# Decay sums of the first mixer: heads on partitions, one picking pass per head instead of four turnings

## The chip, the cores and the metric

The kernel runs on one core of one Trainium2 chip. The metric is the device time of one execution in microseconds (us), as the median over several runs. A core has a matrix engine (TensorE, PE in the rows, with its weight loads shown apart as PEld), a vector engine (DVE), a scalar engine (ACT), GpSimd (POOL), and queues that start transfers (SP).

## The reference, cut to what matters

The program is a chain of layers over 512 tokens of width 1024. The part that the change touches is the first layer's mixer (a state-space mixer with 32 heads in 4 groups, and 4 chunks of 128 tokens). For each head the cumulative sum of `da` inside a chunk is needed twice, as a column over the tokens `l` and as a row over the tokens `s`:

```python
dt = jax.nn.softplus(dt.astype(jnp.float32) + dt_bias.astype(jnp.float32))
a = -jnp.exp(a_log.astype(jnp.float32))
da = dt * a.reshape(g_, r_)
a_cs = jnp.cumsum(da, axis=2)
decay = segsum_exp(jnp.moveaxis(da, 2, -1))     # exp(cs[l] - cs[s]) for s <= l
cb = jnp.einsum('bclgn,bcsgn->bcgls', cm, bm)
y_diag = jnp.einsum('bcgls,bcgrls,bcsgrp->bclgrp', cb, decay, xdt)
```

## The kernel before

Every large product is made in float32 precision out of three passes of the faster fp32r type: each operand is split into a high part (rounded by ACT) and a low part (what is left, subtracted by DVE), and `passes` (the line L699 in the rows) issues high times high, high times low and low times high. A pass moves 512 columns against a stationary block of 128x128.

The first mixer runs at the start, in this order on PE. The input x is turned and split. The raw `dt` of all heads comes out of one block of 24 passes. For group 0 the block "B" follows, then `turn_dt` (four turnings that bring `dt` to tokens on partitions), the block "C", and `decay_sums`: eight small float32 matmuls that give `acs` (cumulative sums, tokens on partitions, a column for each head) and `tot` (chunk totals). Then come the four blocks of x features, four z tiles, the states and the outputs. Groups 1 to 3 do the same without the `dt` parts. The work order is written out by hand in `ssd_group(g)`; each engine runs its own list in order and waits on semaphores. The eight PSUM banks are handed out by the table in `Banks`: `claim` makes PE wait until the bank's last user has freed it.

Between the blocks PE fills in `spread_sums(j)`, one for each of the group's eight heads j: it turns a head's column of `acs`, repeated over 128 columns, four times (once for each chunk), so that PSUM holds the sums as a row on all 128 partitions. ACT's `exp_diff(j)` reads that bank and makes the exponentials of the differences, and DVE's `weights(j)` multiplies them by `CBm`. The places matter below: `spread_sums(0)` and `(1)` stand behind block x0 (and ahead of the sixteen turnings of `y_turn` in groups 1 to 3), `(2)` and `(3)` behind block x1, `(4)` behind block x3 and ahead of `x_turn(1)`, `(5)` behind `x_turn(1)` and ahead of z tile 0, `(6)` and `(7)` behind `x_turn(2)` and `x_turn(3)`. `x_turn` is four turnings.

`spread_sums(5)` claims bank 4, whose user before it is "CB", the products of B and C. DVE frees that bank when it has written `CBm` (L2258). On DVE this stands behind the conv taps of block x2 and the low parts of z, and those stand behind ACT's high parts of z (L1473).

At the start ACT's list is: softplus of `dt`, the exponential of `a_log` (L1494), the high parts of both x halves (L1482, eight pieces), three exponentials of the sums (L1498 to L1500), and the conv starts of B and C (L1526). DVE's list is: `da` (L2186), the copies of `acs` and `tot` (L2188, L2190), their difference (L2192), the low parts of both x halves (L2160, eight pieces), then the conv taps of B and C (L2227).

Of the kernel before, what the change touches and what calls it, by code (L numbers as in the profile page):

```python
# [7 lines left out]
ALU = mybir.AluOpType  # L8
ACT = mybir.ActivationFunctionType
AX = mybir.AxisListType  # L10
F32 = mybir.dt.float32
# [5 lines left out]
P = 128  # L17
T = 512
NT = T // P
# [16 lines left out]
S_HEADS, S_P, S_GROUPS, S_N = 32, 64, 4, 128  # L36
# [28 lines left out]
C_ID, C_TRI, C_ONE, C_MASK = 0, P, 2 * P, 3 * P  # L65
# [66 lines left out]
def build(nc, x, p, cst, par_a, par_b, w_ssd, w_dt, dt_bias, a_log, d_skip, w_ssd_out, w_hgrn, w_hgrn_out,  # L132
          ln_g, ln_b, w_mlp1, w_mlp2, w_gate, w_proj, mem, pos, w_mla, w_uq, w_ukv, w_mem, w_mla_out, fin_g, out):
    with ExitStack() as ctx:
# [16 lines left out]
        con = sb("con", [P, C_ALL])  # L151
# [4 lines left out]
        pT_base = nc.sbuf_base - 4 * DEPTH * KP * T  # L156
# [6 lines left out]
        psum = ctx.enter_context(nc.psum_tensor("psum", [P, 8, HALF], F32))  # L163
        tri = con[:, C_TRI:C_TRI + P]
# [4 lines left out]
        def carve(*shape):  # L169
            n = int(np.prod(shape))  # L170
            assert at[0] + n <= ARENA, (at[0], n)
            v = arena[:, at[0]:at[0] + n]
            at[0] += n
            if len(shape) == 2:
                v = v.rearrange("p (a b) -> p a b", a=shape[0])
            if len(shape) == 3:
                v = v.rearrange("p (a b c) -> p a b c", a=shape[0], b=shape[1])
            return v
# [20 lines left out]
        small = carve(5, S_HEADS)  # L199
        dbias, aneg, dskip, dtmp, _ = [small[:, n, :] for n in range(5)]  # L200
        dt_all = carve(NT, S_HEADS)
        da = carve(NT, S_HEADS)
        acs = carve(NT, S_HEADS)
        tot = carve(NT, S_HEADS)
        decay_end = carve(NT, S_HEADS)
# [16 lines left out]
        def part(name, first, *shape):  # L222
            return nc.alloc_sbuf_tensor_at(name, [P, *shape], F32R, offset=arena_base + 4 * first)

        def over(name, base, *shape):
            return nc.alloc_sbuf_tensor_at(name, [P, *shape], F32R, offset=base)
# [5 lines left out]
        z_his = [part(f"z_hi{n}", ring_first + n * KD * 256, KD, HALF) for n in range(2)]  # L232
        yT_hi = [over("yT_hi_a", fT_base, KD, T), part("yT_hi_b", 0, KD, T)]
        yT_lo = [part("yT_lo_a", 13824, KD, T), part("yT_lo_b", 9728, KD, T)]
        wdt_hi, wdt_lo = part("wdt_hi", xdt_first, KD, P), part("wdt_lo", xw_first, KD, P)

        def ssd_parts(g, unit):
# [98 lines left out]
        bank_full = [sem(f"bank_full{b}") for b in range(8)]  # L336
        bank_free = [sem(f"bank_free{b}") for b in range(8)]
# [14 lines left out]
        def sig(name):  # L352

            if name not in named:
                named[name] = sem(name)
            return named[name]


        banks = Banks()
        banks.stage("start", [("par", 0), ("par_b", 1)] + [(("x", t, h), 2 + (2 * t + h) % 4) for t in range(NT) for h in range(2)])  # L360
        banks.stage("dt", [("dt", 4), ("dtt", 5), ("acs", 6), ("tot", 7)])
        for g in range(S_GROUPS):
            last = g == S_GROUPS - 1
            banks.stage(f"ssd{g}", [("B", 0), ("C", 1), (("x", 0), 2), (("acs", 0), 4), (("acs", 1), 5)]
# [289 lines left out]
        def _(pe):  # L654
# [7 lines left out]
            def turn(b, cols, src, kp=P, mp=P):  # L662

                return pe.transpose(psum[0:mp, b, cols:cols + kp], src, con[0:kp, C_ID:C_ID + kp])  # L664
# [38 lines left out]
            for t in range(NT):  # L703
                pe.wait_ge(x_in[t], 16)
                for h in range(2):
                    b = claim("start", ("x", t, h))
                    for c in range(4):
                        m = turn(b, c * P, x_rows[:, t, (4 * h + c) * P:(4 * h + c + 1) * P])
                    m.then_inc(bank_full[b], 1)
            wait_features("start", lambda t, h: ("x", t, h))  # L710
            b = claim("dt", "dt")
            for k in range(KD):
                if k % 2 == 0:
                    pe.wait_ge(sig("wdt_low"), k // 2 + 1)
                m = passes(psum[:, b, :], (wdt_hi[:, k, :], wdt_lo[:, k, :]), (in_hi[:, k, :], in_lo[:, k, :]), k == 0, k == KD - 1)
            m.then_inc(bank_full[b], 1)
            pe.wait_ge(par_in, 32)
            b = claim("start", "par")
            turn(b, 0, s_par[0:A_ROWS, 0, :], A_ROWS).then_inc(bank_full[b], 1)
            b = claim("start", "par_b")  # L720
# [11 lines left out]
            def decay_sums():  # L732

                pe.wait_ge(sig("da_ready"), 1)
                for name, left in (("acs", tri), ("tot", ones)):
                    b = claim("dt", name)
                    for t in range(NT):
                        m = pe.matmul(psum[:, b, t * S_HEADS:(t + 1) * S_HEADS], left, da[:, t, :], start=True, stop=True)
                    m.then_inc(bank_full[b], 1)

            def y_turn(stage, g):

# [7 lines left out]
            def ssd_group(g):  # L750
# [16 lines left out]
                def spread_sums(j):  # L767

                    b = claim(stage, ("acs", j))
                    h = g * S_HPG + j  # L770
                    for t in range(NT):
                        m = turn(b, t * P, acs[:, t, h:h + 1].broadcast_to([P, P]))
                    m.then_inc(bank_full[b], 1)

                def x_turn(mm_):

# [23 lines left out]
                    decay_sums()  # L800
                feature_block(("x", 0), "x01", x01, 0, True)
                if g == 0:
                    pe.wait_ge(sig("sums_ready"), 1)
                spread_sums(0)
                spread_sums(1)
                if g:
# [6 lines left out]
                b = claim(stage, "CB")  # L813
                for t in range(NT):
                    m = pe.matmul(psum[:, b, t * P:(t + 1) * P], BT[:, t * P:(t + 1) * P], CT[:, t * P:(t + 1) * P],
                                  start=True, stop=True)
                m.then_inc(bank_full[b], 1)
                b = claim(stage, "BT")
                for t in range(NT):
                    m = turn(b, t * P, BT[:, t * P:(t + 1) * P])  # L820
# [18 lines left out]
                for c in range(NT - 1):  # L839
                    if c == 0:  # L840
                        pe.wait_ge(sig("xw_ready"), g * 4 + 4)
                    b = claim(stage, ("st", c))
# [387 lines left out]
            for c in range(2):  # L1230
                b = claim("memkv", ("k", c))
                for k in range(KD):
                    m = pe.matmul(psum[:, b, 0:NMEM], w[:, k, c * P:(c + 1) * P], memT[:, k, :], **first_and_last(k, KD))
# [4 lines left out]
            for m_ in range(MT):  # L1238
                b = claim("memkv", ("v", m_))
                for k in range(KD):  # L1240
                    m = pe.matmul(psum[:, b, 0:MEM_W], memT[:, k, m_ * P:(m_ + 1) * P], w[:, k, MEM_W:2 * MEM_W],
                                  **first_and_last(k, KD))
# [109 lines left out]
            for t in range(NT):  # L1352
                b = claim("first_scores", ("next_s", t))
# [67 lines left out]
            for par in range(2):  # L1421
                h = A_HEADS - 2 + par
# [17 lines left out]
        def _(act):  # L1440
# [18 lines left out]
            for t in range(NT):  # L1459
                for h in range(2):  # L1460
                    b = full("start", ("x", t, h))
# [5 lines left out]
            def ssd_high(g, unit):  # L1467

                hi = ssd_parts(g, unit)[0]
                if unit == "z":  # L1470
                    act.wait_ge(units_landed[1], LAND * (g + 1))
                    for k in range(KD):
                        act.copy(hi[:, k, :], as_k(slots[1])[:, k, :]).then_inc(sig("ssd_high"), 1)  # L1473
                    return
                if unit == "bc":
                    act.wait_ge(bc_in, 32 * (g + 1))
                    raw = bc_w
                else:
                    act.wait_ge(units_landed[0], LAND * (g + 1))
                    raw = as_k(slots[0])[:, :, 0:256] if unit == "x01" else as_k(slots[0])[:, :, 256:512]  # L1480
                for n in range(4):
                    act.copy(hi[:, 2 * n:2 * n + 2, :], raw[:, 2 * n:2 * n + 2, :]).then_inc(sig("ssd_high"), 1)  # L1482
# [9 lines left out]
            act.activation(sp2, sp2, ACT.Ln, bias=1.0)  # L1492
            act.wait_ge(ssd_small_in, 48)
            act.activation(aneg, aneg, ACT.Exp).then_inc(sig("softplus_ln"), 1)  # L1494
            ssd_high(0, "x01")
            ssd_high(0, "x23")
            act.wait_ge(sig("sums_ready"), 1)
# [251 lines left out]
            for i in range(DEPTH):  # L1749
                for k in range(KP):  # L1750
                    b = full("p_turn", ("p", i, k))
# [203 lines left out]
            for c in range(2):  # L1955
                b = full("memkv", ("k", c))
                act.copy(kmT[:, c, :], psum[:, b, 0:NMEM]).then_inc(bank_free[b], 1)
            mla_high(2)
            for m_ in range(MT):
                b = full("memkv", ("v", m_))  # L1960
# [27 lines left out]
            for c in range(2):  # L1988
                b = full("qm", c)
# [130 lines left out]
        def _(dve):  # L2120
            def full(stage, name, i=0):
                return wait_full(dve, stage, name, i)
# [15 lines left out]
            for t in range(NT):  # L2138
                for h in range(2):
                    b = banks.at("start", ("x", t, h))[0]  # L2140
# [10 lines left out]
            def ssd_low(g, unit):  # L2151

                hi, lo = ssd_parts(g, unit)
                raw = {"bc": bc_w, "x01": as_k(slots[0])[:, :, 0:256], "x23": as_k(slots[0])[:, :, 256:512],
                       "z": as_k(slots[1])}[unit]
                step = 1 if unit == "z" else 2
                for n in range(KD // step):
                    ks = slice(step * n, step * n + step)
                    dve.wait_ge(sig("ssd_high"), ssd_split(g, unit, n))
                    dve.tensor_tensor(lo[:, ks, :], raw[:, ks, :], hi[:, ks, :].bitcast(F32),  # L2160
                                      ALU.subtract).then_inc(sig("ssd_low"), 1)

            ssd_low(0, "bc")
            b = full("dt", "dt")
            dve.tensor_copy(dtT[DT_ROW:P, :], psum[DT_ROW:P, b, :]).then_inc(sig("dt_rows"), 1)
            dve.sem_inc(bank_free[b], 1)
            b = full("start", "par")
            dve.tensor_copy(col_a[:], psum[:, b, 0:A_ROWS]).then_inc(bank_free[b], 1)
            b = full("start", "par_b")
# [3 lines left out]
            def heads_on_all(v):  # L2173
                return v.unsqueeze(1).broadcast_to([P, NT, S_HEADS])
# [5 lines left out]
            b = full("dt", "dtt")  # L2180
# [2 lines left out]
            dve.scalar_tensor_tensor(dt_all, sp1, 0.0, sp2, ALU.max, ALU.add)  # L2183
            dve.tensor_scalar(aneg, aneg, -1.0, None, ALU.mult)
            dve.drain()
            dve.tensor_tensor(da, dt_all, heads_on_all(aneg), ALU.mult).then_inc(sig("da_ready"), 1)  # L2186
            b = full("dt", "acs")
            dve.tensor_copy(acs, chunk_heads(b)).then_inc(bank_free[b], 1)  # L2188
            b = full("dt", "tot")
            dve.tensor_copy(tot, chunk_heads(b)).then_inc(bank_free[b], 1)  # L2190
            dve.drain()
            dve.tensor_tensor(decay_end, tot, acs, ALU.subtract).then_inc(sig("sums_ready"), 1)  # L2192
            ssd_low(0, "x01")
            ssd_low(0, "x23")

# [128 lines left out]
            for c in range(NT):  # L2324
                b = banks.at("ssd_out", ("yt", c))[0]
# [605 lines left out]
            for par in range(2):  # L2931
                h = A_HEADS - 2 + par
# [149 lines left out]
```

## Time and profile before

| what | value |
|---|---|
| median of 3 runs | 1921.58 us (1920.56 to 1922.81) |
| the profiled execution, its own time | 1922.01 us |
| its span in the trace | 1920.2 us |
| PE busy | 1881.6 us, 98% of the span |
| PE weight loads busy | 1582.8 us, 82% |
| DVE busy | 1119.9 us, 58% |
| ACT busy | 925.4 us, 48% |

The span is what the trace covers, from the first to the last instruction; the time of an execution has 1.8 us more around it. The chain of work that ended last is on PE for 85% of the span. The four groups of the first mixer lie between about 22 and 330 us.

A row of a timeline gives the start, the duration, the engine, the line and operation, what is written and read, and how many instructions were merged into the row. Matmuls overlap in the records, because one begins before the one ahead of it has left the array: what one costs is read from start to start. A float32 matmul that isn't a turning shows as two records.

### The profile page before, as it was taken

To read this page: it belongs to the slowest core of one execution; us is meant where nothing else is said; L and a number is where in the kernel's file an instruction comes from. 1 tells how busy PE (TensorE), PEld (TensorE's weight loads), DVE (VectorE), ACT (ScalarE), POOL (GpSimd) and SP (SyncE) were. 2 spreads that over 40 slices of the span, in tenths; PEclk is the share of its full clock that TensorE was granted. 3 is DMA by queue.
4 is the path that set the end of the run, shared out by engine and by line. 5 is a ranking of instruction groups with operands and counts; after the bars stand their busy time and mean duration, and the time that the engine had idled before them with its cause. 6 is when DMAs were issued, how large, how long until landed. Compare 5 with 4: busy or idle time off the path is not lost.

```text
span 1920.2 us, 27141 instructions
## 1 busy us (share of the span) xinstructions
PE 1881.6 (98%) x9766; PEld 1582.8 (82%) x9766; DVE 1119.9 (58%) x2000; ACT 925.4 (48%) x1835; POOL 175.8 (9%) x137
## 2 busy tenths in 40 slices
PE   7999999999999999999999999999999999999998
PEld 6787887787888888789998977888888879887986
DVE  4577665645443444657777876534444587456765
ACT  4755756335333324446767655424233365435551
POOL 0101102022000000400100004000000120001100
PEclk9999999999999999999999999999999999999999
DMA  6121313414222232213312114322332232320001
GB/s 205 45 66 45 110 45 110 154 66 153 89 88 87 103 115 88 88 45 89 88 44 64 47 66 152 111 88 87 106 112 88 88 100 80 124 100 1 1 0 44
DMA packets 117634, 162.41 MB, mean 85 GB/s; under 512 B 6085, under 2 KB 58147, under 8 KB 117539
## 3 DMA queue, kind: packets, MB, share of 16 engines
q1 hardware_dynamic: 116243, 156.43, 24.5%
q0 software_dynamic: 1296, 4.72, 0.7%
q8 instruction: 59, 0.97, 0.2%
q14 instruction: 36, 0.29, 0.1%
HBM read 159.03 MB, written 2.10 MB: 84 GB/s over the span
## 4 chain that ended last, share of the span: by engine, by line
PE 85%; DVE 6%; ACT 5%; DVEq 2%; issue 1%; ACTq 0%; DMA 0%; SPq 0%
PE psum L902 49%; PE psum L699 16%; PE psum L1076 5%; PE psum L664 5%; PE psum L1109 2%; PE psum L1338 2%; PE psum L848 1%; DVE z_lo L2160 1%; DVE w_lo L2374 1%; DVEq L2638 1%; PE psum L996 1%; ACT w_hi L1786 1%; DVE w_lo L2209 1%; DVE arena L2227 1%; PE psum L843 0%
## 5 line engine op out<-in xcount | busy, mean ns | idle before, releaser
L2374 DVE TENSOR_TENSOR w_lo<-slot,w_hi 128x512 fp32r<-128x512 f32 x304 | 213.7, 718 | 380.0 <-ACT w_hi L1625 379.9
L1625 ACT CAST w_hi<-slot 128x512 fp32r<-128x512 f32 x304 | 184.8, 621 | 432.9 <-PE psum L902 415.2
L902 PE MATMUL psum<-f_lo,w_hi 128*128 128x512 f32 x528 | 206.1, 390 | 0.0
L902 PE MATMUL psum<-f_hi,w_hi 128*128 128x512 f32 x512 | 200.6, 392 | 4.4 <-DVE f_lo L2381 3.8
L902 PE MATMUL psum<-f_hi,w_lo 128*128 128x512 f32 x512 | 199.7, 390 | 0.0
L902 PE MATMUL psum<-w_hi,hid_hi 128*128 128x512 f32 x512 | 199.5, 390 | 0.0
L902 PE MATMUL psum<-w_hi,hid_lo 128*128 128x512 f32 x512 | 199.2, 389 | 0.0
L902 PE MATMUL psum<-w_lo,hid_hi 128*128 128x512 f32 x512 | 199.2, 389 | 0.0
L2981 POOL TENSOR_TENSOR res<-rn,gb 128x1024 f32<-128x1024 f32 x16 | 43.7, 2732 | 854.1 <-DVE rn L2362 854.1
L902 PEld LDWEIGHTS psum<-f_hi,w_hi 128*128 128x128 f32 x512 | 96.5, 188 | 26.0 <-DVE f_lo L2381 4.6
L902 PEld LDWEIGHTS psum<-f_lo,w_hi 128*128 128x128 f32 x528 | 99.6, 189 | 20.8 <-issue 0.2
L902 PEld LDWEIGHTS psum<-f_hi,w_lo 128*128 128x128 f32 x512 | 96.5, 189 | 20.1
L902 PEld LDWEIGHTS psum<-w_hi,hid_hi 128*128 128x128 f32 x512 | 96.1, 188 | 19.9
L902 PEld LDWEIGHTS psum<-w_hi,hid_lo 128*128 128x128 f32 x512 | 96.1, 188 | 20.0
L902 PEld LDWEIGHTS psum<-w_lo,hid_hi 128*128 128x128 f32 x512 | 96.1, 188 | 19.7
L664 PE MATMUL psum<-con,arena 128*128 128x128 f32 (+1 forms) x614 | 86.2, 274 | 4.9 <-DVE arena L2258 3.3
L664 PEld LDWEIGHTS psum<-con,arena 128*128 128x128 f32 (+1 forms) x614 | 71.8, 144 | 13.5 <-DVE arena L2258 4.2
L902 PE MATMUL psum<-w_hi,f_lo 128*128 128x512 f32 (+2 forms) x224 | 82.9, 370 | 0.0
L699 PE MATMUL psum<-in_hi,ring 128*128 128x512 f32 x192 | 78.7, 410 | 2.4 <-DVE x_lo L2160 1.5
L699 PE MATMUL psum<-in_lo,ring 128*128 128x512 f32 x192 | 76.0, 396 | 0.0
L2227 DVE SCALAR_TENSOR_TENSOR arena<-psum,col_a,arena 128x511 f32<-128x511 f32 (+2 forms) x72 | 53.5, 747 | 30.2 <-ACT arena L1526 26.7
L1076 PE MATMUL psum<-w_hi,f_hi 128*128 128x256 f32 x224 | 65.0, 290 | 0.0
(374 smaller groups left out, 4371.1 us busy)
## 6 DMA issues: line engine op xcount, KB each, us to landing
slot<-in_w_mlp SPq DMA_DIRECT2D x128, 512.0 KB, 5.7
slot<-in_w_ssd SPq DMA_DIRECT2D x32, 512.0 KB, 5.6
slot<-in_w_hgrn SPq DMA_DIRECT2D x32, 512.0 KB, 6.7
slot<-in_w_ssd_out SPq DMA_DIRECT2D x16, 512.0 KB, 6.1
slot<-in_w_gate SPq DMA_DIRECT2D x16, 512.0 KB, 5.3
gb<-in_w_ssd SPq DMA_DIRECT2D x8, 512.0 KB, 8.2
slot<-in_w_hgrn_out SPq DMA_DIRECT2D x8, 512.0 KB, 5.5
slot<-in_w_mla SPq DMA_DIRECT2D x8, 512.0 KB, 5.2
```

Of the source, the lines that this page charges most:

```text
L664: return pe.transpose(psum[0:mp, b, cols:cols + kp], src, con[0:kp, C_ID:C_ID + kp])
L699: m = pe.matmul(out, a, m_, start=first and n_pass == 0, stop=last and n_pass == 2)
L848: m = pe.matmul(psum[:, b, j * S_P:(j + 1) * S_P], Mh[:, j, c * P:(c + 1) * P], xdt[:, c, j * S_P:(j + 1) * S_P], start=True, stop=True)
L902: m = pe.matmul(psum[:, bank[c], cols or slice(0, width)], a, m_, start=opens and k == 0 and n_pass == 0, stop=closes and k == KD - 1 and ...
L996: m = pe.matmul(psum[:, b, :], f_part[:, k, 0:P], w_part[:, k, :], start=n_pass == 0 and k == 0, stop=n_pass == 2 and k == KD - 1)
L1076: m = pe.matmul(out, a, m_, start=k == 0 and n_pass == 0, stop=k == KD - 1 and n_pass == 2)
L1109: m = pe.matmul(psum[:, b, c * P:(c + 1) * P], a, a, start=True, stop=True)
L1338: m = pe.matmul(psum[:, b, (t - 1) * V_HEAD:t * V_HEAD], probT[:, (t - 1) % 2, c * P:(c + 1) * P], values(c), **first_and_last(c, nk))
L1625: act.copy(w_hi[:, k, :], as_k(slot_of(stage, n))[:, k, :]).then_inc(high_made, 1)
L2227: m = dve.scalar_tensor_tensor(cv[:, n % 3, back:T], psum[:, b, 0:T - back], col_a[:, at_:at_ + 1], cv[:, n % 3, back:T], ALU.mult, ALU.add)
L2374: dve.tensor_tensor(w_lo[:, k, :], as_k(slot_of(stage, n))[:, k, :], w_hi[:, k, :].bitcast(F32), ALU.subtract).then_inc(low_made, 1)
L2981: pool.tensor_tensor(res[:, t, :], rn[:, t, :], gb[:, 0, :], ALU.mult).then_inc(sig("res_scaled"), 1)
```

## The change

`da` is now written twice side by side (`da_twice`, 64 columns for each chunk), so that a matmul with it as the stationary operand gives the cumulative sums with heads on 64 partitions, each head twice. That is the new bank use "acsT", four float32 matmuls in `decay_sums`. ACT rounds the 64 rows to fp32r (`sums_parts`), and DVE overwrites the lower 32 rows with what the rounding left, so rows 0 to 31 are high parts and rows 32 to 63 low parts. `picks` is a 64x32 table with two ones in each column. A head's sums are then spread by one fp32r pass: its column of `picks`, repeated over 128 columns, is the stationary operand (64 rows), and `sums_parts` (64 rows, 512 columns) moves. Thus 128 turnings become 32 passes.

```diff
@@ banks
-        banks.stage("dt", [("dt", 4), ("dtt", 5), ("acs", 6), ("tot", 7)])
+        banks.stage("dt", [("dt", 4), ("dtt", 5), ("acs", 6), ("tot", 7), ("acsT", 4)])
@@ PE, decay_sums
+                b = claim("dt", "acsT")
+                for t in range(NT):
+                    m = pe.matmul(psum[0:2 * S_HEADS, b, t * P:(t + 1) * P],
+                                  da_twice[:, t, :], tri, start=True, stop=True)
+                m.then_inc(bank_full[b], 1)
@@ PE, spread_sums
-                    for t in range(NT):
-                        m = turn(b, t * P, acs[:, t, h:h + 1].broadcast_to([P, P]))
-                    m.then_inc(bank_full[b], 1)
+                    pe.matmul(psum[:, b, :], picks[0:2 * S_HEADS, h:h + 1].broadcast_to([2 * S_HEADS, P]),
+                              sums_parts[0:2 * S_HEADS, :], start=True, stop=True).then_inc(bank_full[b], 1)
@@ PE, group 0 before spread_sums(0)
-                    pe.wait_ge(sig("sums_ready"), 1)
+                    pe.wait_ge(sig("sums_low"), 1)
@@ ACT, behind the exponential of a_log
             act.activation(aneg, aneg, ACT.Exp).then_inc(sig("softplus_ln"), 1)
+            b = full("dt", "acsT")
+            act.copy(sums_parts[0:2 * S_HEADS, :], psum[0:2 * S_HEADS, b, :]).then_inc(sig("sums_high"), 1)
             ssd_high(0, "x01")
@@ DVE
+            dve.tensor_tensor(da_twice[:, :, S_HEADS:], dt_all, heads_on_all(aneg), ALU.mult)
             dve.tensor_tensor(da, dt_all, heads_on_all(aneg), ALU.mult).then_inc(sig("da_ready"), 1)
...
             dve.tensor_tensor(decay_end, tot, acs, ALU.subtract).then_inc(sig("sums_ready"), 1)
+            b = full("dt", "acsT")
+            half = slice(S_HEADS, 2 * S_HEADS)
+            dve.tensor_tensor(picks[0:2 * S_HEADS, :], con[0:2 * S_HEADS, C_ID:C_ID + S_HEADS],
+                              con[0:2 * S_HEADS, C_ID + S_HEADS:C_ID + 2 * S_HEADS], ALU.add)
+            dve.wait_ge(sig("sums_high"), 1)
+            dve.tensor_tensor(sums_parts[half, :], psum[half, b, :], sums_parts[half, :].bitcast(F32), ALU.subtract)\
+                .then_inc(sig("sums_low"), 1)
+            dve.sem_inc(bank_free[b], 1)
             ssd_low(0, "x01")
```

The lists of the engines show where the new steps stand. ACT at the start of group 0, before the change (the CAST rows are the high parts: ring_54 of B and C, ring_55 and ring_56 of the two x halves):

```order
L1492 ACTIVATE arena<-arena 128x128
L1494 ACT_TABLE_LOAD
L1494 ACTIVATE arena<-arena 128x32 [waits ssd_small_in]
L1482 CAST ring_55<-slot 128x512 [waits units_landed0]
L1482 CAST ring_55<-slot 128x512 x3
L1482 CAST ring_56<-slot 128x512 [waits units_landed0]
```

The same place of ACT in the changed kernel, whose line numbers are a few higher:

```order
L1498 ACTIVATE arena<-arena 128x128
L1500 ACT_TABLE_LOAD
L1500 ACTIVATE arena<-arena 128x32 [waits ssd_small_in]
L1502 CAST sums_parts<-psum 64x512 [waits bank_full4]
L1488 CAST ring_55<-slot 128x512 [waits units_landed0]
L1488 CAST ring_55<-slot 128x512 x3
L1488 CAST ring_56<-slot 128x512 [waits units_landed0]
```

All high parts of x now stand behind a wait for bank 4, which the last of the new matmuls of `decay_sums` fills. These matmuls on PE, between block C and block x0 of group 0, in the changed kernel (the row L740 is `acs` and `tot`, L744 is the new "acsT"; the rows of before are the same without L744):

```order
L701 MATMUL psum<-in_hi,bc_lo 128x512
L740 MATMUL psum<-arena,con 128x32 [waits da_ready]
L740 MATMUL psum<-arena,con 128x32 x7
L744 MATMUL psum<-con,arena 64x128 [waits bank_free4]
L744 MATMUL psum<-con,arena 64x128 x3
L701 MATMUL psum<-in_hi,ring_55 128x512 [waits ssd_low,bank_free2]
```

They stand ahead of block x0. PE between block x3 and z tile 0 of group 0, before the change (the rows are `spread_sums(4)`, `x_turn(1)` and `spread_sums(5)`, all turnings):

```order
L664 MATMUL psum<-con,arena 128x128 [waits bank_free7]
L664 MATMUL psum<-con,arena 128x128 x3
L664 MATMUL psum<-con,arena 128x128 [waits bank_free5,conv_silu]
L664 MATMUL psum<-con,arena 128x128 x3
L664 MATMUL psum<-con,arena 128x128 [waits bank_free4]
L664 MATMUL psum<-con,arena 128x128 x3
L699 MATMUL psum<-z_hi_57,in_hi 128x512 [waits ssd_low,bank_free2]
```

The same place in the changed kernel:

```order
L778 MATMUL psum<-sums_parts,picks 128x512 [waits bank_free7]
L666 MATMUL psum<-con,arena 128x128 [waits bank_free5,conv_silu]
L666 MATMUL psum<-con,arena 128x128 x3
L778 MATMUL psum<-sums_parts,picks 128x512 [waits bank_free4]
L701 MATMUL psum<-z_hi_57,in_hi 128x512 [waits ssd_low,bank_free2]
```

Each group of four turnings of `acs` has become one pass with 64 rows, which stands between turnings and full passes with 128 rows; the wait for bank 4 is where it was.

## Rows read from the trace of the kernel before

**Rows 1.** The page, busy time by engine (share of the span, number of instructions).

```profile
PE 1881.6 (98%) x9766; PEld 1582.8 (82%) x9766; DVE 1119.9 (58%) x2000; ACT 925.4 (48%) x1835; POOL 175.8 (9%) x137
```

**Rows 2.** Waits of PE, 0 to 480 us: total, times, longest (us).

```profile
PE psum L664 <- DVE arena L2258: 3.3, 4, 1.7
```

**Rows 3.** Timeline of PE, group 0, `spread_sums(0)` and `(1)` between x0 and x1.

```profile
44.74 0.40 PE L699 MATMUL psum<-in_hi,x_lo 128*128 128x512 f32 x1
44.97 1.03 PE L664 MATMUL psum<-con,arena 128*128 128x128 f32 x8
45.77 0.48 PE L699 MATMUL psum<-in_hi,ring 128*128 128x512 f32 x1
46.09 0.40 PE L699 MATMUL psum<-in_lo,ring 128*128 128x512 f32 x1
```

**Rows 4.** Timeline of PE, group 1: `spread_sums(4)` with `x_turn(1)`, then `spread_sums(5)`.

```profile
143.12 0.40 PE L699 MATMUL psum<-in_hi,x_lo 128*128 128x512 f32 x1
143.36 1.04 PE L664 MATMUL psum<-con,arena 128*128 128x128 f32 x8
144.91 0.65 PE L664 MATMUL psum<-con,arena 128*128 128x128 f32 x4 [0.51 <-DVE arena L2258]
```

**Rows 5.** Timeline of PE in the last layer: turnings, 64-row matmul (L1297), full passes.

```profile
1727.39 0.39 PE L664 MATMUL psum<-con,arena 128*128 128x128 f32 x2
1727.71 0.70 PE L1297 MATMUL psum<-arena 64*128 64x256 f32 x2
1728.34 0.50 PE L699 MATMUL psum<-ukv_hi,ckvT_hi 128*128 128x512 f32 x1
1728.68 0.39 PE L699 MATMUL psum<-ukv_lo,ckvT_hi 128*128 128x512 f32 x1
```

**Rows 6.** Timeline of PE's weight loads, behind the 64-row matmul.

```profile
1728.34 0.19 PEld L699 LDWEIGHTS psum<-ukv_hi,ckvT_hi 128*128 128x128 f32 x1 [0.33 <-issue]
```

**Rows 7.** Timeline of PE in the last layer: turnings, then fp32r passes of 96 rows.

```profile
1764.87 0.61 PE L664 MATMUL psum<-con,arena 128*128 128x128 f32 x4
1765.23 0.47 PE L699 MATMUL psum<-kT_hi,qT_hi 96*128 96x512 f32 x1
1765.55 0.40 PE L699 MATMUL psum<-kT_lo,qT_hi 96*128 96x512 f32 x1
```

**Rows 8.** Timeline of PE, group 0: the 32-row turnings of `turn_dt` between passes.

```profile
28.08 0.40 PE L699 MATMUL psum<-in_hi,bc_lo 128*128 128x512 f32 x1
28.41 0.43 PE L728 MATMUL psum<-con,arena 32*128 32x32 f32 x4
28.77 0.50 PE L699 MATMUL psum<-in_hi,ring 128*128 128x512 f32 x1
29.11 0.40 PE L699 MATMUL psum<-in_lo,ring 128*128 128x512 f32 x1
```

**Rows 9.** Timeline of PE, group 0: `decay_sums`, and the first pass of x0.

```profile
34.45 1.87 PE L738 MATMUL psum<-arena,con 128*128 128x32 f32 x16
37.77 0.47 PE L699 MATMUL psum<-in_hi,ring 128*128 128x512 f32 x1 [1.46 <-DVE x_lo L2160]
```

**Rows 10.** Timeline of ACT, group 0.

```profile
33.06 4.24 ACT L1482 CAST ring<-slot 128x512 fp32r<-128x512 f32 x8
...
38.00 1.64 ACT L1526 ACTIVATE arena<-psum,col_a 128x512 f32<-128x512 f32 x2
...
46.48 0.63 ACT L1532 ACTIVATE arena<-arena 128x512 f32<-128x512 f32 x1 [1.67 <-DVE arena L2227]
...
64.48 0.58 ACT L1566 COPY arena<-psum 128x512 f32<-128x512 f32 x1
```

**Rows 11.** Timeline of DVE, group 0: low parts of x, then the taps of B.

```profile
36.94 4.90 DVE L2160 TENSOR_TENSOR x_lo<-slot,ring 128x512 fp32r<-128x512 f32 x8
41.76 4.68 DVE L2227 SCALAR_TENSOR_TENSOR arena<-psum,col_a,arena 128x511 f32<-128x511 f32 x6
```

**Rows 12.** Windows: stretch, length, busy us of each engine, PE clock (1.00 is full), DMA.

```profile
37.80:45.00 7.20, 7.20 (x25) 5.67 (x26) 6.98 (x12) 3.59 (x5) 0.00 (x0) 0.76 0.56 146
47.20:66.00 18.80, 18.80 (x99) 15.74 (x98) 10.32 (x16) 17.83 (x37) 0.00 (x0) 1.00 0.01 2
```

More of the change, by code:

```diff
@@ L201, in build @@
         dt_all = carve(NT, S_HEADS)
-        da = carve(NT, S_HEADS)
+        da_twice = carve(NT, 2 * S_HEADS)
+        da = da_twice[:, :, 0:S_HEADS]
         acs = carve(NT, S_HEADS)
@@ L234, in build @@
         yT_lo = [part("yT_lo_a", 13824, KD, T), part("yT_lo_b", 9728, KD, T)]
+        sums_parts, picks = over("sums_parts", pT_base, T), over("picks", pT_base + 4 * T, S_HEADS)
         wdt_hi, wdt_lo = part("wdt_hi", xdt_first, KD, P), part("wdt_lo", xw_first, KD, P)
```

## The prediction

> **What bounds the kernel now.** I read the busy shares first: PE works for 98% of the span [rows 1], so what PE spends from start to start counts, unless it stands at a place where PE waits anyway. The waits of PE come next. Inside the four groups of the first mixer PE stops at one place in each group, for the bank that DVE's `CBm` frees, 3.3 us in all and 1.7 at most [rows 2]. The timeline shows that place: `spread_sums(5)` of group 1 begins at 144.91 after 0.51 us idle [rows 4]. Groups 2 and 3 take (3.3 - 1.7 - 0.5) / 2, again about half a microsecond each, so the 1.7 is group 0's. What PE saves or loses ahead of that place is swallowed as long as DVE comes last there; what stands behind it counts in full. Third comes the start of group 0, where PE waits 1.46 us for the low part of x [rows 9] and where the new steps on ACT and DVE stand.
>
> **What a spread costs now.** Eight turnings run from 44.97 to 45.77: 0.80 us, 0.10 each [rows 3]. Full passes follow each other at 0.23 (44.74 to 44.97). The first pass behind turnings is followed at 0.32 (45.77 to 46.09), so leaving the turnings costs 0.09 more. A spread is thus 0.40 us of PE.
>
> **What a spread costs after.** No pass of 64 rows in fp32r exists in the trace. The lower bound is the full pass, 0.23. A pass of 96 rows behind four turnings behaves like a full one: it begins 0.36 after the turnings do and is followed at 0.32 [rows 7]. The nearest row in shape is the 64-row matmul of the last layer. Two turnings ahead of it take 0.32 (1727.39 to 1727.71) where 0.20 is normal; the matmul, two records that I count as nearly a full pass each (0.22), takes 0.63 until the full pass starts, and that one is followed at 0.34 (1728.34 to 1728.68) [rows 5]. Together 1.29, against 0.20 + 0.44 + 0.23 = 0.87 without friction: **0.42 us for going to 64 rows and back**. The weight load behind it shows why: it starts with its own matmul, after 0.33 us idle of "issue" [rows 6], whereas loads between full passes run in the shadow of the matmul ahead. The 32-row turnings of `turn_dt` show the same: 28.08 to 28.77 and 0.34 after [rows 8]; with their own issue at about 0.07 each ((0.43 - 0.23) / 3), the 1.03 us hold 0.23 + 0.27 + 0.23 and 0.30 of friction. I take 0.40, near the row of the same row count, and keep 0.30 and 0.09 (only leaving turnings) as ends.
>
> The Trainium skill, "TensorEngine Tiling (Array Packing)", section "Key Properties", says that a change of tiling mode drains the engine, and its list of modes has 64 and 32 rows but no 96. By that rule every spread pays a drain on both sides, which agrees with the rows on 64, 32 and 96 rows above and speaks against this change; the sum by it is the forecast below.
>
> **PE, place by place.**
> - `spread_sums(5)`, `(6)`, `(7)`: each is followed by a z tile and stands behind four turnings. Before: 0.40 and the 0.09 of leaving. After: 0.23 + 0.40 = 0.63, and the 0.09 is in it. Worked directly from rows 5: four turnings 0.52, one record less than 0.63 is 0.41, then 0.34: 1.27 instead of 0.80 + 0.32 = 1.12. That is **+0.15** each. All three stand at or behind the CB wait: 12 x 0.15 = **+1.8 us**.
> - `spread_sums(4)`, between a full block and turnings: +0.23; `(2)` and `(3)`, a pair between full blocks: 0.46 + 0.40 against 0.89, -0.03; `(0)` and `(1)` in groups 1 to 3, a pair ahead of sixteen turnings: 0.86 against 0.80, +0.06. Ahead of the wait they only make PE later, by 0.2 to 0.3, and the wait is 0.51 [rows 4]: they cost nothing, except that the last of them makes block x1 and with it ACT's chain later: 3 x 0.06 = **+0.2 us**. Were the wait gone, they would cost 0.26 a group more, 1 us in all.
>
> The Trainium skill, "TensorE: Matmul & The Clock Gate", section "LDWEIGHTS (loading the stationary operand)", says that a weight load's time goes with its columns and not with its rows. Taken alone it would let a 64-row pass cost what a full pass does; the load row above stays at 0.19 us, as it says, but starts late. That is rival A.
>
> **The start of group 0.** ACT now waits for "acsT" ahead of all high parts of x. `acs` and `tot` are sixteen records in 1.87 us, the last starting at about 36.2 [rows 9]. The new four matmuls are eight records more. With 0.11 each (1.87 / 16 is the nearest row) their results are there at 37.2; with a drain for their 64 columns, priced like half of the 0.4 above, at 37.4. ACT's copy is 64x512; a copy of 512 columns takes 0.58 [rows 10] with the next start about 0.5 later. So the casts begin at 37.75 to 37.95 instead of 33.06: 4.7 to 4.9 us later. The conv of B, at 38.00 before, follows 4.94 behind the casts' start: 42.7 to 42.9, and is done 0.8 later, at about 43.55. The taps of B on DVE began at 41.76, straight behind the low parts of x [rows 11]; now they wait for that conv and begin at about 43.6. The low parts themselves follow the new subtraction and are no later than this (38.7 + 4.9 = 43.6). So both lists give a shift of 1.85 us. ACT waits for those taps (the row at 46.48, 1.67 idle [rows 10]), so its own 3 us of slack end there. From 47.2 to 66.0 ACT is busy 17.83 of 18.80 us [rows 12] with no wait in between: the shift reaches the z casts, DVE's `CBm` and PE's wait unbroken: **+1.85 us**. DVE's second `da` (0.2 us, before `da_ready`) hides behind block C, which holds PE until 34.45 [rows 9]; the extra matmuls hide in the 1.46 us of idle; `picks` hides in DVE's wait for ACT's copy.
>
> Block x0 itself starts about 1.6 us later than 37.77 (first cast 38.4, first low part 39.3). That is less than the 1.85 and is swallowed at the CB wait. At 37.8 to 45.0 the granted clock averaged 0.76 [rows 12] after PE's thin stretch and idle; the stretch becomes 1.6 us longer. PE arrives at group 0's wait with 1.8 us to spare, so a further microsecond at the lower level (1.2 instead of 2.4 GHz) costs nothing.
>
> **The sum.** 1.85 + 1.8 + 0.2 = 3.85, say +3.9 us. The profiled execution took 1922.01, so 1925.9; the median lies 0.43 below it, so **1925.5 us**. PE has 88 records fewer (128 turnings go, 32 passes and 8 records come), and yet the time grows.
>
> **Rivals.**
> - **A, the 64-row pass costs a full pass (25%).** For it: the row above is a float32 matmul in another place, and 96 rows pay nothing. Against: two row counts in three places show the friction. Then (5) to (7) give 0.23 - 0.40 = -0.17 each, -2.0 us; the pair ahead of `y_turn` brings x1 and ACT's chain 0.34 forward in three groups, -1.0; what the rest saves goes into the CB wait. With the start's +1.85: -1.2 us, **1920.4 us**. It turns on the friction: with f per spread excursion the sum is 1.85 + 12 (f - 0.25) + 3 (f - 0.34), zero at f = 0.14 us.
> - **B, friction as expected, but the late ACT list at the start is absorbed (12%).** It would be, if "acsT" were there soon enough for ACT; against: ACT stood idle 0 us between L1494 and the casts, and the casts must wait 4.7 us. Then +2.0, **1923.6 us**.
> - **C, friction costs more (8%).** If fp32r loads (0.19) behind or ahead of 64 rows cost 0.1 more each, and the CB wait is used up: 0.15 more for 12 spreads, and some at (4): +6, **1927.6 us**.
> - **D, A with the start absorbed too (3%)**: -3.0, **1918.6 us**.
> The forecast itself has 52%, with its own range from f = 0.30 (+1.85 + 0.6 = 2.5) to +5: 1924.1 to 1926.6.
>
> **The numbers.** The range reaches from A to between the forecast and C: 1920.0 to 1927.0. 0.2% is 3.84 us, about what a measurement of this kernel can tell from no change. The forecast lies just at that bound: 0.30 of its 0.52 and all of C are slower, 0.38; D, where its start's gain comes out larger still, and a corner of A are faster, 0.03; the rest is 0.59.
>
> **What would show it.** In the trace after: `picks` passes at 0.6 us or so from start to start of the next full pass instead of 0.23, with idle "issue" ahead of the weight loads on both sides; the eight ring casts at about 37.8 on ACT; the taps of B at 43.6; group 0's CB wait at about 1.8 us and those of groups 1 to 3 at about 0.3; the groups half a microsecond further apart than before. Weight loads of `picks` in the shadow of the pass ahead, or conv starts at 38 as before, would make it wrong.

## The result and the profile after

The changed kernel took 1925.45 us in the median of 20 runs, against 1922.22 us for the kernel before: a ratio of 1.0019 with a 95% interval of 1.0013 to 1.0026. It is 3.2 us slower in the medians (2.5 to 5.0 by the interval), inside the predicted range of 1920.0 to 1927.0 and at the predicted 1925.5. One of the 20 runs, of 9742.36 us, is counted as slow and is not in the ratio.

The two profiled executions did not reach the decay sums at the same time: 34.45 us in the kernel before, 32.54 in the changed one, mostly because the `dt` block, which the change does not touch, ran at the full clock in one and partly at the lower level in the other (from 15 to 20 us the granted clock was 0.73 before and 1.00 after): 7.21 us against 5.67. That is luck of the execution, and it is why the two traced executions (1922.01 and 1923.78) differ by only 1.8 us. So every time inside the first mixer is counted here from the start of the decay sums. The end mark is the first state matmul of group 3, which waits 0.93 us for the same line of ACT in all kernels. These are the rows of before (L738, L843) and after (L740, L849), from the timelines of PE:

```profile
324.32 2.81 PE L843 MATMUL psum<-arena 128*128 128x512 f32 x6 [0.93 <-ACT arena L1582]
```

```profile
32.54 1.87 PE L740 MATMUL psum<-arena,con 128*128 128x32 f32 x16
34.34 1.09 PE L744 MATMUL psum<-con,arena 128*64 128x128 f32 x8
37.63 0.77 PE L701 MATMUL psum<-in_hi,ring 128*128 128x512 f32 x1 [2.20 <-DVE x_lo L2168]
...
326.18 2.81 PE L849 MATMUL psum<-arena 128*128 128x512 f32 x6 [0.93 <-ACT arena L1590]
```

With 34.45 of [rows 9], the stretch is 289.87 us before and 293.64 after: +3.77 us. This "mixer stretch" is the measure for the experiments, beside the medians; behind it the traced executions differ by up to 1.6 us from that of before, without a pattern. Each stretch comes from one execution.

The start of group 0, after. ACT (first fence) copies the sums at 35.46 and begins the high parts at 35.95, which is 3.41 us behind the decay sums; before, it began them 1.39 us ahead of them [rows 9, 10]. DVE (second fence) has the taps of B at 41.73, that is 9.19 behind the decay sums instead of 7.31: +1.88 us, with 1.85 predicted. Both lists are ready for them at the same time, as predicted: the conv of B, begun at 40.90, takes 0.8, and the low parts end at 41.70.

```profile
35.46 0.58 ACT L1502 CAST sums_parts<-psum 64x512 fp32r<-64x512 f32 x1 [4.21 <-PE psum L744]
35.95 4.26 ACT L1488 CAST ring<-slot 128x512 fp32r<-128x512 f32 x8
...
46.46 0.63 ACT L1540 ACTIVATE arena<-arena 128x512 f32<-128x512 f32 x1 [1.67 <-DVE arena L2244]
...
53.12 0.78 ACT L1534 ACTIVATE arena<-psum,col_a 128x512 f32<-128x512 f32 x1 [0.40 <-issue]
```

```profile
36.79 4.91 DVE L2168 TENSOR_TENSOR x_lo<-slot,ring 128x512 fp32r<-128x512 f32 x8
41.73 4.70 DVE L2244 SCALAR_TENSOR_TENSOR arena<-psum,col_a,arena 128x511 f32<-128x511 f32 x6
...
67.53 0.68 DVE L2275 TENSOR_TENSOR arena<-psum,con 128x512 f32<-128x512 f32 x1
```

The `CBm` row of the kernel before, from the timeline of DVE:

```profile
67.23 0.68 DVE L2258 TENSOR_TENSOR arena<-psum,con 128x512 f32<-128x512 f32 x1
```

`CBm` of group 0 comes at 32.78 before and 34.99 after: +2.21. That is 0.33 more than the taps of B. The reader finds it in ACT's row at 53.12: 0.40 us of idle with "issue" as its releaser, ahead of the conv start of x1, where the kernel before has none. The last experiment below is about it.

The spreads, after, from the timeline of PE in group 1: number 4 with `x_turn(1)`, the CB wait (PE waits ahead of number 5 for the bank that `CBm` frees) and number 5, then number 6 behind `x_turn(2)`.

```profile
143.80 0.40 PE L701 MATMUL psum<-in_hi,x_lo 128*128 128x512 f32 x1
144.13 0.50 PE L778 MATMUL psum<-sums_parts,picks 64*128 64x512 f32 x1
144.55 0.66 PE L666 MATMUL psum<-con,arena 128*128 128x128 f32 x4
145.62 0.50 PE L778 MATMUL psum<-sums_parts,picks 64*128 64x512 f32 x1 [0.41 <-DVE arena L2275]
146.05 0.50 PE L701 MATMUL psum<-z_hi,in_hi 128*128 128x512 f32 x1
146.39 0.39 PE L701 MATMUL psum<-z_lo,in_hi 128*128 128x512 f32 x1
...
151.70 0.60 PE L666 MATMUL psum<-con,arena 128*128 128x128 f32 x4
152.23 0.49 PE L778 MATMUL psum<-sums_parts,picks 64*128 64x512 f32 x1
152.65 0.50 PE L701 MATMUL psum<-z_hi,in_hi 128*128 128x512 f32 x1
152.99 0.39 PE L701 MATMUL psum<-z_lo,in_hi 128*128 128x512 f32 x1
```

And the weight loads of the last three (PEld):

```profile
152.23 0.18 PEld L778 LDWEIGHTS psum<-sums_parts,picks 64*128 64x128 f32 x1 [0.17 <-issue]
152.65 0.19 PEld L701 LDWEIGHTS psum<-z_hi,in_hi 128*128 128x128 f32 x1 [0.24 <-issue]
```

Both loads start with their own matmul and after idle time, into the 64 rows and out of them. From 151.70 to 152.99 four turnings, the spread and one full pass take 1.29 us. Without friction they would take 0.40 + 0.23 + 0.23 = 0.86, so this visit to 64 rows costs 0.43 us. The kernel before needs 1.12 for eight turnings and a pass [rows 3].

### The profile page after: what moved, and what is told of

Read it like the earlier page. It is cut to its first block, busy times and chain, and to the rows that moved or that the text cites. A ratio compares the mean times of both kernels' runs of the same rounds, so it can differ in the third digit from the quotient of the medians.

```text
span 1922.0 us, 26970 instructions
## 1 busy us (share of the span) xinstructions
PE 1883.6 (98%) x9678; PEld 1573.3 (82%) x9678; DVE 1121.4 (58%) x2003; ACT 925.7 (48%) x1836; POOL 175.8 (9%) x137
## 4 chain that ended last, share of the span: by engine, by line
PE 85%; DVE 6%; ACT 5%; DVEq 2%; issue 1%; DMA 0%; ACTq 0%; SPq 0%
PE psum L908 49%; PE psum L701 16%; PE psum L1082 5%; PE psum L666 4%; PE psum L1115 2%; PE psum L1344 2%; PE psum L854 1%; DVE z_lo L2168 1%; DVE w_lo L2391 1%; DVEq L2655 1%; PE psum L1002 1%; ACT w_hi L1794 1%; DVE w_lo L2226 1%; DVE arena L2244 0%; PE psum L849 0%
## 5 line engine op out<-in xcount | busy, mean ns | idle before, releaser
L666 PE MATMUL psum<-con,arena 128*128 128x128 f32 (+1 forms) x486 | 70.9, 274 | 1.7 <-DVE yT_lo_b L2344 1.3
L666 PEld LDWEIGHTS psum<-con,arena 128*128 128x128 f32 (+1 forms) x486 | 57.2, 146 | 9.7 <-issue 5.1
```

## The experiments

My theory: (a) going to 64 rows and back costs PE about 0.4 us a visit, which is more than the spread saves; (b) ACT's list at the start delays group 0; (c) what PE saves or loses ahead of the CB wait is swallowed. The rivals were that the friction belongs to something other than the row count, and that one of the two costs makes up the whole loss.

The table gives the median, the ratio of this kernel to the kernel before with its 95% interval, and the mixer stretch of the traced execution against 289.87 us of the kernel before. Each stretch is the difference of two rows like those above.

| kernel | median us | ratio, interval | stretch, difference |
|---|---|---|---|
| changed kernel | 1925.45 | 1.0019, 1.0013 to 1.0026 | 293.64, +3.77 |
| start_only | 1924.25 | 1.0011, 1.0002 to 1.0020 | 292.12, +2.25 |
| rows96 | 1920.35 | 0.9993, 0.9984 to 1.0002 | 288.91, -0.96 |
| rows128 | 1920.44 | 0.9994, 0.9985 to 1.0003 | 288.89, -0.98 |
| late_copy | 1925.16 | 1.0015, 1.0006 to 1.0024 | 294.12, +4.25 |
| late_again | 1924.99 (one run) | none | 292.77, +2.90 |
| rows128_late | 1921.18 | 0.9993, 0.9984 to 1.0002 | 287.86, -2.01 |
| cb_later | 1918.88 | 0.9985, 0.9976 to 0.9994 | 286.34, -3.53 |
| all_three | 1914.67 | 0.9960, 0.9947 to 0.9974 | 283.27, -6.60 |
| one_more_act | 1922.87 (one run) | none | 290.23, +0.36 |

### The start alone

```diff
-                    pe.matmul(psum[:, b, :], picks[0:2 * S_HEADS, h:h + 1].broadcast_to([2 * S_HEADS, P]),
-                              sums_parts[0:2 * S_HEADS, :], start=True, stop=True).then_inc(bank_full[b], 1)
+                    for t in range(NT):
+                        m = turn(b, t * P, acs[:, t, h:h + 1].broadcast_to([P, P]))
+                    m.then_inc(bank_full[b], 1)
```

> The changed kernel with the old spreads: all new steps at the start stay (second da, acsT, ACT's copy ahead of the high parts of x, the subtraction and its wait), but spread_sums turns a column of acs four times as before. My theory: the start alone costs 1.9 us through ACT's late list, and 0.3 more because the longer low-clock stretch makes block x1 late: +2.2 us against the kernel before, ratio 1.0011. Rival 'absorbed': the late list is hidden and the 64-row passes cost everything: 0, ratio 1.0000. Rival 'all of it': the passes cost nothing net: +3.3, ratio 1.0017.

Measured: +2.25 us in the stretch, a ratio of 1.0011. The start costs 2.2 of the 3.8 us and the passes the rest, 1.5. The rival "absorbed" (0) and the rival "all of it" (+3.3 in the medians, which is +3.8 in the stretch) both fall by the trace; the interval of the times alone would not exclude the second. The 0.3 that I put down to the clock is wrong, as one_more_act shows below.

### 96 and 128 rows

```diff
-                    pe.matmul(psum[:, b, :], picks[0:2 * S_HEADS, h:h + 1].broadcast_to([2 * S_HEADS, P]),
-                              sums_parts[0:2 * S_HEADS, :], start=True, stop=True).then_inc(bank_full[b], 1)
+                    pe.matmul(psum[:, b, :], picks[0:96, h:h + 1].broadcast_to([96, P]),
+                              sums_parts[0:96, :], start=True, stop=True).then_inc(bank_full[b], 1)
...
             dve.memset(eps_h[:], RMS_EPS).then_inc(sig("eps_set"), 1)
+            dve.memset(sums_parts[2 * S_HEADS:96, :].bitcast(F32), 0.0)
```

> The changed kernel with picks and sums_parts used over 96 partitions, rows 64 to 95 zero, so the spread pass has 96 rows and computes the same. My theory (going to 64 rows and back costs about 0.4 us a visit): weight loads run in the shadow again, spreads 5 to 7 cost 0.23 instead of 0.56 to 0.63, the groups lie 76.1 us apart instead of 77.3; with the start's +2.2 the time is 0.9 us below the kernel before, 4 us below the changed kernel: ratio 0.9995. Rival: the friction belongs to fp32r passes between float32 turnings, or to the repeated column of picks, not to the row count: no change against the changed kernel, ratio 1.0018.

The second kernel has 128 in place of 96.

> The changed kernel with picks and sums_parts over all 128 partitions, rows 64 to 127 zero. My theory: same as with 96 rows, since both stay in the full array: 0.9 us below the kernel before, ratio 0.9995. Rival: the cost grows or falls with rows, so that 128 differs from 96 by more than 0.5 us.

Measured: -0.96 and -0.98 us in the stretch, 4.7 us below the changed kernel. The same place of group 1 with 96 rows, PE and its weight loads:

```profile
147.32 0.49 PE L778 MATMUL psum<-sums_parts,picks 96*128 96x512 f32 x1 [1.13 <-DVE arena L2276]
...
153.24 0.60 PE L666 MATMUL psum<-con,arena 128*128 128x128 f32 x4
153.60 0.47 PE L778 MATMUL psum<-sums_parts,picks 96*128 96x512 f32 x1
153.91 0.39 PE L701 MATMUL psum<-z_hi,in_hi 128*128 128x512 f32 x1
154.14 0.40 PE L701 MATMUL psum<-z_lo,in_hi 128*128 128x512 f32 x1
```

```profile
153.57 0.19 PEld L778 LDWEIGHTS psum<-sums_parts,picks 96*128 96x128 f32 x1
153.68 0.19 PEld L701 LDWEIGHTS psum<-z_hi,in_hi 128*128 128x128 f32 x1
```

Four turnings, the spread and one pass take 0.90 us (153.24 to 154.14) instead of 1.29, and both loads start ahead of their matmuls. Type, repeated column and neighbours are those of the changed kernel, so the 0.39 us is the row count's. With 128 rows the same place takes 0.90 us too (151.81 to 152.71): 32 or 64 rows of zeros cost nothing that shows. The row at 147.32 shows theory (c): the wait for `CBm` is now 1.13 us instead of 0.41, so what PE saved with the spreads ahead of it is lost there again. From +2.25 (start_only) to -0.96 the cheap passes bring 3.2 us, and the start takes 2.2 of them. The medians tell both kernels from the changed one, but not from the kernel before.

### The copy behind the high parts

```diff
@@ ACT
-            b = full("dt", "acsT")
-            act.copy(sums_parts[0:2 * S_HEADS, :], psum[0:2 * S_HEADS, b, :]).then_inc(sig("sums_high"), 1)
             ssd_high(0, "x01")
             ssd_high(0, "x23")
+            b = full("dt", "acsT")
+            act.copy(sums_parts[0:2 * S_HEADS, :], psum[0:2 * S_HEADS, b, :]).then_inc(sig("sums_high"), 1)
@@ DVE (picks is made earlier)
+            ssd_low(0, "x01")
             b = full("dt", "acsT")
             half = slice(S_HEADS, 2 * S_HEADS)
             dve.wait_ge(sig("sums_high"), 1)
             dve.tensor_tensor(sums_parts[half, :], psum[half, b, :], sums_parts[half, :].bitcast(F32), ALU.subtract)\
                 .then_inc(sig("sums_low"), 1)
             dve.sem_inc(bank_free[b], 1)
-            ssd_low(0, "x01")
             ssd_low(0, "x23")
```

> The changed kernel with ACT's copy of the sums moved behind the eight high parts of x, DVE's subtraction moved between the two halves of the low parts, and picks made before the softplus. Spreads keep 64 rows. My theory: ACT's casts begin straight behind the exponential of a_log again, the taps of B shift by 0.6 us (the subtraction) instead of 1.9, and block x0's idle is 1.5 us as before: 1.5 us below the changed kernel, about +1.8 against the kernel before, ratio 1.0009. Rival 'the start costs nothing': same as the changed kernel, 1.0018.

Measured: the stretch is +4.25, no better than the changed kernel, although the taps of B came 8.26 us behind the decay sums (42.99 - 34.73) instead of 9.19. My 0.6 for their shift was too small, it is 0.95. The second `da` (0.21 us) has no part in it: DVE's low parts begin 2.50 behind the decay sums, 2.49 in the kernel before. The subtraction takes 0.72 from start to start (39.75 to 40.47), and the low parts, cut in two runs of four, take 2.52 each instead of 4.82 for all eight, 0.22 more. The rest of the miss stands in PE's rows at z tile 0 of this kernel, and in the windows around them (here the busy time of PE alone, its clock, DMA):

```profile
69.50 0.66 PE L778 MATMUL psum<-sums_parts,picks 64*128 64x512 f32 x1 [1.63 <-DVE arena L2276]
70.09 0.80 PE L701 MATMUL psum<-z_hi,in_hi 128*128 128x512 f32 x1
70.68 0.63 PE L701 MATMUL psum<-z_lo,in_hi 128*128 128x512 f32 x1
```

```profile
68.00:70.00 2.00, 0.50 (x1) 0.92 0.00 0
70.00:72.00 2.00, 2.00 (x6) 0.50 0.00 0
72.00:74.00 2.00, 2.00 (x8) 0.73 0.51 101
```

Behind two waits of 2.6 and 1.6 us the granted clock fell to 0.50, that is 1.2 instead of 2.4 GHz, and the first passes of z tile 0 followed each other at 0.43 instead of 0.23. A second execution of the same kernel was traced:

> The same kernel as late_copy, looked at once more. There z tile 0 of group 0 ran at the lower TensorE level after 2.6 and 1.6 us of PE idle and took 6.8 us instead of 5.4, which ate the 0.95 us by which CBm came earlier. If that belongs to this kernel's idle, it shows again and the g3 states start some 4.2 us later than in the kernel before; if it was this one execution, the states start about 2.8 us later.

```profile
70.06 0.50 PE L778 MATMUL psum<-sums_parts,picks 64*128 64x512 f32 x1 [1.64 <-DVE arena L2276]
70.48 0.50 PE L701 MATMUL psum<-z_hi,in_hi 128*128 128x512 f32 x1
70.82 0.39 PE L701 MATMUL psum<-z_lo,in_hi 128*128 128x512 f32 x1
```

This time the clock stayed and the stretch was +2.90, with 2.8 expected for that case. So the repair is worth 0.9 us where the clock stays, and one execution lost more than that (1.35) to the clock behind the same waits. Idle time alone does not decide it: in the trace of rows128_late, below, PE waits 3.40 and 1.98 us at the same two places, and the granted clock stays at 1.00. The medians (1925.16 and 1925.45) do not tell the repair from nothing.

### Both repairs, and the CB wait

The first kernel here joins the 128 rows and the late copy.

> Both repairs: 128 rows for the spreads and the late copy (ACT's copy behind the high parts, the subtraction between the low halves, picks early). My theory: the two costs are independent and add: start +0.6 to 0.8, spreads -3.1: 2.4 us below the kernel before, ratio 0.9988. Rival: the group-0 wait for CBm swallows one of them: no better than either repair alone, 0.9995.

Measured: -2.01 in the stretch, 1.03 below rows128, so the two costs add, as expected (-2.4 with the too small 0.6). In the medians it does not show: 1921.18 is even above the 1920.44 of rows128, the ratio is 0.9993 as with 96 rows, and the interval is wider than the gain.

The second changes the kernel before alone:

```diff
                 x_turn(1)
-                spread_sums(5)
                 z_tile(0)
+                spread_sums(5)
                 x_turn(2)
```

> The kernel before with one change: spread_sums(5) stands behind z tile 0 instead of ahead of it, so PE no longer waits there for DVE's CBm. My theory: this wait is real idle time of PE, 0.5 us in three groups and 1.7 in the first, and nothing else is due at once: -3.0 us, ratio 0.9984. Rival: PE arrives earlier at another wait (the silu of x2 for x_turn(2), or exp_diff(4) for bank 7) and gives it back: between -1 and 0, ratio 0.9996 or more.

Measured: -3.53 in the stretch, a ratio of 0.9985. The CB wait was real idle time, and more of it than the 0.51 in its rows, which count from the modelled end of the turnings ahead. From start to start, eight turnings that take 0.80 [rows 3] take 1.55 up to number 5 in group 1 (143.36 to 144.91 [rows 4]), so PE lost 0.75, and from one group's `CBm` to the next cb_later is 0.72 us shorter. In groups 1 to 3 no other wait replaces it; in group 0 ACT's exp_diff of head 4 is waited for a little (timeline of PE):

```profile
71.56 0.32 PE L664 MATMUL psum<-con,arena 128*128 128x128 f32 x1 [0.35 <-ACT rn L1538]
...
146.97 1.47 PE L664 MATMUL psum<-con,arena 128*128 128x128 f32 x12
148.20 0.48 PE L699 MATMUL psum<-z_hi,in_hi 128*128 128x512 f32 x1
```

The third kernel joins everything.

> Both repairs and spread_sums(5) behind z tile 0. My theory: without the CBm wait everything that PE saves in a group counts, 1.5 us in each of four groups, and the wait itself goes, 0.5 three times and 1.7 once; the late start of ACT's list no longer reaches PE in group 0: 6.0 + 3.2 = 9 us below the kernel before, ratio 0.9953; something else may then be late (x_turn(2) on the silu of x3, or ACT's exp_diff for the banks), which would leave -5 to -6. Rival: the sums do not add at all because ACT's chain bounds each group: -3, 0.9984.

Measured: -6.60 in the stretch, 1914.67 us and a ratio of 0.9960 (0.9947 to 0.9974), **the fastest version here**, and 7.6 us below the kernel before. That is 2.4 us short of the expected 9. From `CBm` to `CBm` each group is 2.0 to 2.1 us shorter than before, 6.1 in three steps, as expected; what lies ahead of the first and behind the last gives only 0.5. In group 0 something else is late, as the reserve in the expectation said, but at another place first: `x_turn(0)` waits 3.38 us for ACT's silu of x0, and number 6 then 0.80 us for the bank of ACT's exp_diff of head 4. The late start still reaches PE there. No run moves `x_turn(0)`, so its share is not shown.

```profile
61.01 0.33 PE L666 MATMUL psum<-con,arena 128*128 128x128 f32 x1 [3.38 <-ACT arena L1540]
```

Once the CB wait is gone, the spreads' saving counts more: the two repairs add 3.1 us to cb_later's 3.5, while without it they brought 2.0.

### One more instruction on ACT

```diff
             act.activation(aneg, aneg, ACT.Exp).then_inc(sig("softplus_ln"), 1)
+            act.copy(dtmp, dbias)
```

> The kernel before plus one small copy on ACT (32 columns, to a tile nobody reads), behind the exponential of a_log, where the changed kernel has its copy of the sums. In every traced kernel with that extra instruction whose group 0 I looked at, ACT stands still 0.40 us ahead of the conv start of x1, with no instruction named as its releaser; in the kernel before it does not. Theory 'position': the gap comes with one more instruction in ACT's list, whatever it waits for, so it appears here too and group 0's CBm comes 0.3 us later than in the kernel before. Rival 'lateness': the gap comes from PE's late block x1 or the late chain, so it does not appear here and CBm's time stays at 32.8 us behind the start of the decay sums.

Measured, from the timelines of ACT and DVE (the decay sums start at 34.95):

```profile
53.65 0.78 ACT L1527 ACTIVATE arena<-psum,col_a 128x512 f32<-128x512 f32 x1 [0.40 <-issue]
```

```profile
68.06 0.68 DVE L2259 TENSOR_TENSOR arena<-psum,con 128x512 f32<-128x512 f32 x1
```

The gap appears, `CBm` stands at 33.11 instead of 32.78, +0.33, and the stretch is 0.36 longer. PE's block x1 is on time here, so the gap does not come from PE's lateness or from the clock: it comes with one more instruction in ACT's list. The same gap of 0.40 us stands in all nine traced executions with that one instruction more, and in neither of the two without it (before and cb_later). The single times (1922.87, and 1922.77 for the kernel before beside it) could not show 0.3 us. The trace names no releaser, and why the place of an instruction in the list matters stays open.

## Why the prediction was right, point by point

**The forecast** was +3.9 us with 64-row friction and a late start, and the trace has +3.77 in the mixer stretch. The medians of 20 runs differ by 3.2. That the median of 1925.45 meets 1925.5 is luck: the forecast was added to 1921.58, the median of 3 runs, and 20 runs of the kernel before gave 1922.22, so 0.64 too little there made up for 0.7 too much in the change.

- **Friction of a visit to 64 rows.** Predicted 0.40 from rows of a float32 matmul in another layer [rows 5, 8]; measured 0.43 on the fp32r pass itself. rows96 showed that it is the row count's, and rival A, without friction, came true only there and with 128 rows: -0.96 and -0.98, with -1.2 worked out.
- **Spreads 5 to 7.** Predicted +0.15 each. Number 6 measures 1.29 against 1.12, +0.17. Number 5 stands behind an idle PE and costs less: from its start to the second pass of z tile 0 it takes 0.77 us (145.62 to 146.39), and before it took 0.72 (0.40 and 0.32), so +0.05. I had charged the full price of going in where nothing was streaming.
- **The pair ahead of `y_turn`** was predicted to make x1 0.06 later. It did not: from ACT's conv start of x0 to that of x1 it is 8.12 us in group 1 (122.36 to 130.48) and was 8.19, so x1 comes 0.07 earlier. From `CBm` to `CBm` the changed kernel takes 77.36, 77.32 and 77.32 us instead of 76.94 or 76.95, and behind the last `CBm` 0.39 more than before: 0.37 to 0.42 a group and not 0.51, 1.56 in all instead of 2.0.
- **The start.** Predicted +1.85, measured +1.88 at the taps of B. It reached the CB wait unbroken, as predicted, and rival B, in which it is absorbed, fell with start_only.
- **ACT's issue gap**, 0.33 us, was in no step. It nearly makes up for what the groups were over-priced by: 1.88 + 0.33 + 1.56 are 3.77, and that the sum came so near is partly luck.
- **The clock.** At 37.8 to 45.0 the granted clock of the changed kernel was 0.60 instead of 0.76 [rows 12]. As predicted it cost nothing, since PE still had time to spare at the CB wait.
- **The swallowing.** Predicted about 0.3 us left of the wait in groups 1 to 3 and 1.8 in group 0; the waits are 0.41 and 0.94. In group 0 the prediction names the further microsecond at the lower clock and does not take it off the 1.8.

So the mechanisms of the forecast were the right ones. Its sum was right within 0.2 us while its terms were off by up to 0.4 us in both directions, and the small pair ahead of `y_turn` had the wrong sign.

## What to carry to other kernels

Count a short matmul by the rows of its stationary block too: a lone pass of 64 rows among full ones cost 0.66 us of which 0.23 was work, and padding it with rows of zeros to 96 or 128 gave 0.39 back at no cost that shows. A copy that only a later step needs does not belong ahead of work that the next block waits for. And before making an engine's work cheaper, look for the one wait behind it: here moving one spread past a tile was worth more (3.5 us) than the repaired change without it (2.0), and raised what the latter brings to 3.1.

## What the runs showed of the hardware

- A change from 128 rows to 64 and back cost 0.43 us, and 96 rows counted as 128 (0.04 us): the weight loads into and out of 64 rows did not run in the shadow of the matmul ahead. The Trainium skill, "TensorEngine Tiling (Array Packing)", section "Key Properties", says that changing the tiling mode drains the engine. The measured rows agree, with the 0.43 us as its size for both ways here.
- With one more ACT instruction of 32 columns a 0.40 us gap stood some 20 us later in ACT's list.
- Behind 2.6 and 1.6 us of PE idle the granted clock fell to 0.50 for some 3 us in one execution and not in the next of the same kernel, nor behind 3.4 and 2.0 us in rows128_late.
